# Moving two subtractions and two multiplications of a recurrent unit from VectorE to GpSimd

## The reference, cut to what matters

```python
def rg_lru(u, w_a, b_a, w_x, b_x, lam):
    ...
    r = jax.nn.sigmoid(jnp.einsum('blgi,gij->blgj', ub, w_a).reshape(bsz, L, LRU_WIDTH) + b_a)
    i = jax.nn.sigmoid(jnp.einsum('blgi,gij->blgj', ub, w_x).reshape(bsz, L, LRU_WIDTH) + b_x)
    log_a = -RG_LRU_C * r * jax.nn.softplus(-lam)
    a = jnp.exp(log_a)
    mult = jnp.sqrt(-jnp.expm1(2.0 * log_a))
    return linear_scan(a, mult * i * uf)
```

## Time and profile before

| | |
|---|---|
| median of 3 runs | 1300.44 us (1299.69 to 1301.47) |
| the profiled execution | 1303.09 us |
| its span, first to last instruction | 1301.2 us |
| PE busy | 1127.3 us, 87% |
| DVE busy | 629.3 us, 48% |
| ACT busy | 453.3 us, 35% |
| POOL busy | 78.4 us, 6% |

### The profile page before, as it was taken

How to read it: one execution, slowest core, us unless ns; L and a number is a source line. 1 busy time by engine, 2 the same in 40 slices (tenths; PEclk the granted TensorE clock), 3 DMA queues, 4 the chain that set the end, 5 groups by cost and what they waited for, 6 DMA issues and landing times.

```text
span 1301.2 us, 19504 instructions
## 1 busy us (share of the span) xinstructions
PE 1127.3 (87%) x8166; PEld 841.6 (65%) x8166; DVE 629.3 (48%) x1168; ACT 453.3 (35%) x835; POOL 78.4 (6%) x118
## 2 busy tenths in 40 slices
PE   5899999999996756799999675669999999999898
PEld 3677758896842312269984231326999779999856
DVE  4655876656520201156753010114885489655584
ACT  3535534322410000044341000002664666533473
POOL 3000224540000000000000000000100000000000
PEclk8999999999997888799999888879999999999999
DMA  9937765119989999995878999999345305454100
GB/s 326 330 129 262 285 230 199 66 43 391 421 353 422 420 421 421 415 325 194 324 305 343 422 419 422 422 417 353 130 150 175 130 1 184 141 194 165 46 2 32
DMA packets 104187, 339.17 MB, mean 261 GB/s; under 512 B 7849, under 2 KB 10774, under 8 KB 81574
## 3 DMA queue, kind: packets, MB, share of 16 engines
q1 hardware_dynamic: 97408, 334.51, 66.3%
q10 hardware_dynamic: 6694, 3.43, 1.0%
HBM read 336.88 MB, written 1.05 MB: 260 GB/s over the span
## 4 chain that ended last, share of the span: by engine, by line
PE 60%; DMA 13%; SPq 11%; DVE 10%; ACT 4%; issue 2%; ACTq 0%; DVEq 0%
PE bank L712 8%; PE bank L714 8%; PE bank L713 8%; SPq L1409 7%; DMA weight_ring<-in_w_up_dram 5%; PE bank L1065 4%; SPq L1420 4%; PE bank L612 3%; DVE arena L2137 3%; DMA arena<-in_w_up_dram 3%; DMA arena<-in_w_gate_dram 3%; PE bank L689 2%; PE bank L570 2%; PE bank L690 2%; DVE weights_low L2137 2%
## 5 line engine op out<-in xcount | busy, mean ns | idle before, releaser
L2137 DVE TENSOR_TENSOR weights_low<-weight_ring,weights_high 128x1024 fp32r<-128x1024 f32 x150 | 183.5, 1225 | 146.5 <-ACT weights_high L1591 146.1
L1591 ACT ACTIVATE weights_high<-weight_ring 128x1024 fp32r<-128x1024 f32 x150 | 158.2, 1056 | 187.9 <-PE bank L714 173.6
L712 PE MATMUL bank<-input_high,weights_high 128*128 128x272 f32 (+1 forms) x672 | 195.3, 291 | 4.7 <-DVE input_low L2137 2.3
L714 PE MATMUL bank<-input_high,weights_low 128*128 128x272 f32 (+1 forms) x672 | 192.0, 286 | 0.0
L713 PE MATMUL bank<-input_low,weights_high 128*128 128x272 f32 (+1 forms) x672 | 191.5, 285 | 0.0
L2137 DVE TENSOR_TENSOR arena<-arena,bank 128x512 f32<-128x512 f32 (+1 forms) x38 | 24.6, 651 | 224.4 <-PE bank L1065 211.0
L712 PEld LDWEIGHTS bank<-input_high,weights_high 128*128 128x128 f32 x672 | 126.7, 189 | 9.1 <-issue 4.9
L714 PEld LDWEIGHTS bank<-input_high,weights_low 128*128 128x128 f32 x672 | 126.9, 189 | 0.0
L713 PEld LDWEIGHTS bank<-input_low,weights_high 128*128 128x128 f32 x672 | 126.7, 189 | 0.1
L712 PE MATMUL bank<-raw_high,weights_high 128*128 128x272 f32 (+1 forms) x320 | 92.5, 289 | 2.0 <-DVE weights_low L2137 2.0
L714 PE MATMUL bank<-raw_high,weights_low 128*128 128x272 f32 (+1 forms) x320 | 91.2, 285 | 0.0
(11 more groups left out here) (467 smaller groups left out, 1969.6 us busy)
## 6 DMA issues: line engine op xcount, KB each, us to landing
weight_ring<-in_ada_w_dram SPq DMA_DIRECT2D x24, 2048.0 KB, 10.2
weight_ring<-in_w_gate_dram SPq DMA_DIRECT2D x16, 2048.0 KB, 24.6
arena<-in_w_down_dram SPq DMA_DIRECT2D x16, 2048.0 KB, 32.7
arena<-in_w_gate_dram SPq DMA_DIRECT2D x12, 2048.0 KB, 21.4
arena<-in_w_up_dram SPq DMA_DIRECT2D x12, 2048.0 KB, 33.0
weight_ring<-in_w_up_dram SPq DMA_DIRECT2D x12, 2048.0 KB, 27.7
weight_ring<-in_even_w_in_dram SPq DMA_DIRECT2D x9, 2048.0 KB, 9.2
expert_slots<-in_w_up_dram SPq DMA_DIRECT2D x8, 2048.0 KB, 32.6
```

The source lines that it names most:

```text
L712: pe.matmul(b[:, 0:width], hi[:, k, :], high[:, k, t0:t0 + width], start=k == 0, stop=False)
L714: mm = pe.matmul(b[:, 0:width], lo[:, k, :], high[:, k, t0:t0 + width], start=False, stop=k == KD - 1)
L1591: act.activation(WHI[:, j % 2], quarter_of(j), ACT.Copy).then_inc(weights_high, 1)
L2137: return dve.tensor_tensor(out_, a, b, op)
```

## The change

GpSimd does the two subtractions and the two multiplications, with the same operands, in its own program behind the masks of the third layer. VectorE no longer does them; its splits stay where they were. A new semaphore, scan_input, tells VectorE's scans that the multiplication of their half is done; ScalarE's exponentials wait for half_ready as before, which GpSimd now signals. GpSimd also waits once for lru_in, the products that VectorE puts into LI.

```diff
@@ -421,6 +421,7 @@
         lc_ready, half_ready = sem("lru_decay_scale_ready"), sem("lru_half_log_ready")
+        scan_input = sem("lru_scan_input_ready")
@@ -1543,6 +1544,16 @@
             keep_if(LATER, [[-1, P]], -1, 1).then_inc(iota_ready, 1)
 
+            pool.wait_ge(lru_in, KD)
+            for half in range(2):
+                v = slice(4 * half, 4 * half + 4)
+                pool.wait_ge(logs_ready, half + 1)
+                pool.tensor_tensor(LTH[:, v], LTH[:, v], LX[:, v], ALU.subtract).then_inc(half_ready, 1)
+            for half in range(2):
+                v = slice(4 * half, 4 * half + 4)
+                pool.wait_ge(mult_ready, half + 1)
+                pool.tensor_tensor(LI[:, v], LI[:, v], LTH[:, v], ALU.mult).then_inc(scan_input, 1)
+
             pool.wait_ge(h_ready, h_count(6))
@@ -2722,12 +2733,6 @@
-            def lru_half(half):
-
-                v = slice(4 * half, 4 * half + 4)
-                dve.wait_ge(logs_ready, half + 1)
-                tt(LTH[:, v], LTH[:, v], LX[:, v], SUB).then_inc(half_ready, 1)
-
             for g in range(2):
@@ -2738,18 +2743,12 @@
             for half in range(2):
-                lru_half(half)
                 split()
 
-            def lru_input(half):
-
-                v = slice(4 * half, 4 * half + 4)
-                dve.wait_ge(mult_ready, half + 1)
-                then(tt(LI[:, v], LI[:, v], LTH[:, v], MUL))
-
             def lru_scan(m):
 
                 dve.wait_ge(lru_decay, m + 1)
+                dve.wait_ge(scan_input, m // 4 + 1)
                 return dve.tensor_tensor_scan(MIX3[:, m, :], LR[:, m, :], LI[:, m, :], 0.0, MUL, ADD)
@@ -2768,8 +2767,6 @@
                 split()
-                if m < 2:
-                    lru_input(m)
                 if 1 <= m <= 4:
```

## The result

| | before | changed |
|---|---|---|
| median | 1302.21 us (20 runs, 1299.69 to 1303.34) | 1303.50 us (20 runs, 1301.20 to 1306.62) |
| the profiled execution | 1303.09 us | 1303.79 us |
| its span | 1301.2 us | 1301.2 us |

Changed to before 1.0014, 95% interval 1.0009 to 1.0020: slower by 1.8 us (1.2 to 2.6). That ratio is an estimate over all runs; the two medians themselves lie 1.3 us apart. The three runs shown ahead of the prediction are among the 20 of before, and the median of the 20 is 1.8 us above theirs.

A forecast was written before the change was run, and what follows sets the result against it. TensorE, waiting on VectorE's low parts and then without idle time behind 1106 us, bounds the kernel. Delays of 1.0 and 3.1 us less 1.3 given back make +1.8 on 1300.44: 1302.2 us, own range 1301.4 to 1303.0, wide 1299.8 to 1303.8.

The forecast's parts named there:

- VectorE's pauses hide the subtractions and the first multiplication: On VectorE, 1073 to 1087 us: removing these gains nothing; removing the second multiplication gains 0.7 us, limited by a high part.
- GpSimd's reads and VectorE's two-SBUF-input instructions take turns: In the stretch's splits and scans: each engine waits for the other's whole instruction; VectorE work with a PSUM input doesn't wait.
- The duration of 2.35 us: Each of the four 128x1088 GpSimd operations was taken as 2.35 us, between 2.23 and 2.47 scaled from 128x512 rows.
- step 1: First subtraction on GpSimd, 1073.4 to 1075.7 us, delays VectorE's first split; the product's first quarter starts 1.0 us late.
- Step 3: On ScalarE, the fourth split's high part waits for the product's second quarter, so that split is asked for 1.0 us late.
- Step 4: Both GpSimd multiplications run back to back ahead of VectorE's fourth split, which ends at 1088.15 us, 3.1 late.
- this case at +2.05: VectorE's fourth split goes first, then the second multiplication gets in before the scans, which start about 1088.35 us: +2.05 us.
- rows 8: GpSimd's select issued at 913.74 us ended after VectorE's run; by it the second multiplication follows the scans, +1.6 us.
- No turns: Rival: in the stretch GpSimd and VectorE don't wait for each other, the gain stays, -0.7 us, 1299.7; chance 0.08.
- The hole: Rival: the second multiplication never stands before VectorE's fourth split, scans or fifth split; +0.3 us, 1300.7; chance 0.10.
- The clock: Rival: longer TensorE idle time lowers its granted clock for 5 us, adding 2.3 us; +4.1, 1304.5; chance 0.05.
- The longer operation: Rival: GpSimd operations last over 2.62 us, slower by over 0.2%; at 2.8 us it is +3.1, 1303.6; chance 0.17.

The follow-up runs named there:

- the additional operations: Kernel before plus four unused GpSimd operations at the changed kernel's moments: subtractions local 39.24 us, ratio 1.0049; memsets of equal length local 33.01 us, ratio 0.9994.
- the last experiments: Kernel before plus four GpSimd 128x128 selects: local 33.05 us; or plus one 128x128 multiplication ahead of the select at 913 us: that multiplication lasted 3.41 us.

## Where the prediction was right, and the steps that failed

- **The step that failed: "on the median 1300.44 + 1.8 = 1302.2".** It took three runs for the level of before, and twenty have it at 1302.21. So the forecast time is the level of before itself, as if nothing changed, while the changed kernel measured 1303.50, 1.3 above the forecast and above its own range (1301.4 to 1303.0), though inside the wide one. The difference was worked out with care and set on a base that was off by as much as the difference. The profiles suggest why three runs are too few: executions with a lower granted clock ahead of the stretch reach it about 3 us later than the others. That the runs without a profile divide in the same way isn't shown.
- **VectorE's pauses hide the subtractions and the first multiplication; the second is worth 0.7.** Right: 0.61 when the multiplications leave the run without a price.
- **GpSimd's reads and VectorE's two-SBUF-input instructions take turns.** Right, and shown by the additional operations: +6.23 us for those that read, 0.00 for those that only write.
- **The duration of 2.35 us.** Too short: 2.54, above both rows scaled by their elements (2.23 and 2.47). This term was mis-sized. With GpSimd's start 0.16 us behind the logarithm, where step 1 had 0.06, it makes quarter 0 1.3 us late instead of 1.0, and quarter 1 1.2.
- **Step 3, the high part of split 3.** Right: ScalarE's copy waited for quarter 1, and split 3 started 1.2 us late (11.73 us from the logarithm's end, 10.52 before).
- **Step 4, both multiplications ahead of split 3.** Wrong in its order: split 3 was asked for about 0.15 us before multiplication 0 ended, and the second one got in behind it, before the scans. So quarter 3 came 1.2 us late and not 2.6. The prediction had this case at +2.05. With 2.54 in place of 2.35 in the two operations that count in it, it would be 2.43; measured is 2.24, mainly because a GpSimd operation that has waited is shorter, too: the second multiplication ends 2.41 us behind its release (1083.37 to 1085.78). Of its two ways to settle the order, the one from the Trainium skill, "SBUF — State Buffer", section "Who interferes with whom", came true here (issue order decides), and the one read from rows 8 did not. In the run at 913 us it is the other way round, as the last experiments show, so neither holds everywhere.
- **The sum.** +1.8 predicted, +2.24 in the stretch, 1.8 (1.2 to 2.6) by the ratio. That the ratio gives the predicted 1.8 is in part luck: the order that made up that 1.8 did not occur, and the stretch lost 0.4 more. Within 0.2%, as the prediction thought likeliest.
- **The rivals.** No turns: fell (rows of 2.51 and 2.44 us for splits). The hole: for multiplication 0 there was one, for multiplication 1 none. The clock: it stayed granted in full in the stretch, with idle times of 1.21 and 1.47 us on TensorE. The longer operation: half true; 2.54 lies between my value and the 2.62 from which 0.2% would have been passed. The 2.39 us estimated in that rival was too short as well.

## What to carry to other kernels

Before moving elementwise work to an idle GpSimd, look at what VectorE does at that moment: an instruction there with both inputs in SBUF waits for the whole GpSimd instruction if that one reads SBUF, so 2.54 us of "free" work cost more than the 1.3 us that it took away. Work moved off an engine is worth only what the next wait leaves of it, and an engine's pauses are the first place to look: a new order on ScalarE and VectorE alone got 0.6 us in the stretch, too little to be seen in the whole kernel's time. Cutting GpSimd's operation into pieces shortens the single wait but multiplies the meetings (+1.66 instead of +2.24).

## What the runs showed of the hardware that was not expected

- A GpSimd tensor_tensor of two full f32 operands takes 2.54 us for 128x1088, more than in proportion to 1.05 or 1.16 us for 128x512 (2.23 and 2.47).
- A run of eight short VectorE subtractions with a split behind it stretched a GpSimd operation of 128x128 to 3.4 us, and a select of 0.29 us to 3.24, while between long instructions it was let in after one.
- GpSimd starts 0.08 to 0.16 us behind the end of the ScalarE instruction that releases it (1073.99 to 1074.07 and 1070.42 to 1070.58 in the changed kernel), VectorE 0.03 us (1073.31 to 1073.34).
- A GpSimd operation that has waited for its turn ends 2.41 us behind its release instead of 2.54 (worked out from the row of 6.09 us), as a VectorE split ends 1.08 us behind it instead of 1.23.
